# Whole 1 MB modulation tiles in a ring of two buffers in place of half tiles in a ring of four

## What is computed

```python
cond = jax.nn.silu(c)
mod = cond @ mod_w[i] + mod_b[i]                     # 2048 x 12288
sh_m, sc_m, gt_m, sh_f, sc_f, gt_f = jnp.split(mod[:, None, :], 6, axis=-1)
h = rms_norm(x, norm_g[i, 0]) * (1.0 + sc_m) + sh_m
y = swa_sink_attention(h, swa_w_qkv[j], swa_w_o[j], swa_sinks[j], cos, sin)
x = x + gt_m * rms_norm(y, norm_g[i, 1])
h = rms_norm(x, norm_g[i, 2]) * (1.0 + sc_f) + sh_f
x = x + gt_f * rms_norm(swiglu(h, ffn_w_in[i], ffn_w_out[i]), norm_g[i, 3])
```

## Time and profile before

| | |
|---|---|
| Median of three runs | 1232.06 us (1229.7 to 1233.01) |
| The profiled execution, its own time | 1226.82 us |
| Its span in the profile | 1225.0 us |
| Granted TensorE clock over the span | 0.933 |
| Busy: TensorE, VectorE, ScalarE, GpSimd | 86%, 64%, 39%, 7% of the span |
| Read from HBM | 286.39 MB, 235 GB/s over the span |

### The profile page before, as it was taken

The page is one execution under the profiler, slowest core; times in us unless marked ns, Lnnn a source line. Parts: engine busy times, 40 slices in busy tenths (PEclk is TensorE's granted clock), DMA queues, the critical chain, the costliest instruction groups (busy, mean ns, idle before and its releaser), DMA issues.

```text
span 1225.0 us, 13423 instructions
## 1 busy us (share of the span) xinstructions
PE 1053.1 (86%) x4712; PEld 862.1 (70%) x4712; DVE 782.4 (64%) x843; ACT 476.7 (39%) x568; POOL 83.5 (7%) x57
## 2 busy tenths in 40 slices
PE   0155568797778996999999999999999999999995
PEld 0144457576656765888888888888888888888884
DVE  5777879999987868476676644444444454454544
ACT  3311232653653444433343433343334434344343
POOL 0000013313311001000000000000000000000002
PEclk9677778798878998999999999999999999999998
DMA  8998877887779962687787755555655455555541
GB/s 310 362 322 308 297 273 249 282 307 274 267 251 341 342 241 68 205 293 265 268 303 278 268 178 194 185 199 176 205 174 201 149 198 202 178 202 194 185 169 69
DMA packets 104194, 288.94 MB, mean 236 GB/s; under 512 B 6752, under 2 KB 6752, under 8 KB 97888
## 3 DMA queue, kind: packets, MB, share of 16 engines
q1 hardware_dynamic: 103152, 286.29, 67.0%
q10 hardware_dynamic: 1008, 2.23, 0.5%
HBM read 286.39 MB, written 2.10 MB: 235 GB/s over the span
## 4 chain that ended last, share of the span: by engine, by line
PE 65%; DVE 16%; DMA 9%; issue 5%; ACT 4%; POOL 1%; ACTq 0%; SPq 0%; DVEq 0%
PE ps L1095 21%; PE ps L1097 21%; PE ps L1096 21%; DMA mraw<-in_mod_w 8%; DVE mraw L580 5%; DVE wlo L569 5%; ACT whi L312 2%; ACT s L368 1%; PE ps L1117 1%; DMA sinkp<-in_sinks 1%; DVE hf L842 1%; DVE qr L648 1%; PE ps L1214 0%; DVE qr L654 0%; PE ps L1234 0%
## 5 line engine op out<-in xcount | busy, mean ns | idle before, releaser
L569 DVE TENSOR_TENSOR wlo<-raw,whi 128x2048 fp32r<-128x2048 f32 x172 | 395.2, 2299 | 312.1 <-ACT whi L312 312.0
L1095 PE MATMUL ps<-whi,hThi 128*128 128x512 f32 x1248 | 497.6, 399 | 94.0 <-DVE wlo L569 88.7
L312 ACT ACTIVATE whi<-raw 128x2048 fp32r<-128x2048 f32 x172 | 328.7, 1913 | 466.5 <-PE ps L1097 455.7
L1096 PE MATMUL ps<-wlo,hThi 128*128 128x512 f32 x1248 | 492.9, 395 | 0.0
L1097 PE MATMUL ps<-whi,hTlo 128*128 128x512 f32 x1248 | 492.5, 395 | 0.0
L1095 PEld LDWEIGHTS ps<-whi,hThi 128*128 128x128 f32 x1248 | 238.9, 191 | 150.7 <-issue 91.1
L1097 PEld LDWEIGHTS ps<-whi,hTlo 128*128 128x128 f32 x1248 | 238.7, 191 | 50.9
L1096 PEld LDWEIGHTS ps<-wlo,hThi 128*128 128x128 f32 x1248 | 239.2, 192 | 49.2
L580 DVE CUSTOM_DVE_ANT_0 mraw<-mraw,cb,modT 128x1024 f32<-128x1024 f32 x96 | 128.7, 1358 | 36.0 <-DMA mraw<-in_mod_w 35.8
L580 DVE CUSTOM_DVE_ANT_0 mraw<-mraw,cb,mbias 128x1024 f32<-128x1024 f32 x96 | 124.3, 1311 | 41.2 <-DMA mraw<-in_mod_w 30.2
L1095 PE MATMUL ps<-whi,oThi 128*128 128x512 f32 x128 | 53.6, 419 | 6.3 <-DVE wlo L569 3.6
(11 more groups left out here) (131 smaller groups left out, 543.6 us busy)
## 6 DMA issues: line engine op xcount, KB each, us to landing
mraw<-in_mod_w SPq DMA_DIRECT2D x192, 512.0 KB, 6.2
raw<-in_w_in SPq DMA_DIRECT2D x88, 1024.0 KB, 5.1
raw<-in_w_out SPq DMA_DIRECT2D x44, 1024.0 KB, 4.8
raw<-in_w_qkv SPq DMA_DIRECT2D x24, 1024.0 KB, 8.7
raw<-in_w_o SPq DMA_DIRECT2D x16, 1024.0 KB, 8.5
x<-in_x ACTq DMA_DIRECT2D x2, 1024.0 KB, 11.9
x<-in_x SPq DMA_DIRECT2D x2, 1024.0 KB, 8.2
out<-x SPq DMA_DIRECT2D x8, 256.0 KB, 2.6
```

The lines of the kernel that those rows point to most:

```text
L312: A(whi[:, s % 2], raw[:, s], ACT.Copy).then_inc(hi_done, 1)
L569: V.tensor_tensor(wlo[:, s % 2], raw[:, s], whi[:, s % 2].bitcast(F32), ALU.subtract).then_inc(lo_done, 1)
L1095: mm(dst, hi, whi[:, s % 2, n], start=start, stop=False)
L1096: mm(dst, hi, wlo[:, s % 2, n], start=False, stop=False)
```

## The change

A modulation piece is a whole tile: one load of 128 rows of 8 KB, one multiply-and-sum over 2048 columns that starts from the bias. A group has four pieces f = 0 to 3. The ring has two buffers of 1 MB. The order written in terms of j stays as it is; a piece f stands where j = 2f stood, and at odd j nothing is done. So f0 to f3 stand at j = 0, 2, 4, 6. The load of a piece waits until VectorE has done the piece two before it. The wait of the second half for the first is gone.

```diff
-MHALF = D // 2
-MPN = 8
-MRING = 4
+MPN = 4
+MRING = 2
...
-        mraw = sb("mraw", [P, MRING, MHALF])
+        mraw = sb("mraw", [P, MRING, D])
...
-        def piece_of(j):
-
-            return 2 * (j // 4) + j % 2, j // 2 % 2
-
...
             def load_m(n, j, col=None, first=False):
 
-                if not first:
-                    sp.wait_ge(acc_step, MPN * n + j - 3)
+                if j % 2:
+                    return
+                f = j // 2
+                if not (first and f < MRING):
+                    sp.wait_ge(acc_step, MPN * n + f - 1)
                 c = n if col is None else col
-                f, half = piece_of(j)
-                src = mod_w[bass.ds(4 * c + f, 1), :, half * MHALF:(half + 1) * MHALF]
-                sp.dma_start(mraw[:, j % 4], src.rearrange("a p k -> p (a k)")).then_inc(m_loaded[j % 4], 16)
+                src = mod_w[bass.ds(4 * c + f, 1)].rearrange("a p k -> p (a k)")
+                sp.dma_start(mraw[:, f % 2], src).then_inc(m_loaded[f % 2], 16)
...
             def mod(n, j, col=None):
 
-                f, half = piece_of(j)
+                if j % 2:
+                    return
+                f = j // 2
                 c = n if col is None else col
                 dst = modT[:, bass.ds(4 * c + f, 1)]
-                dve.wait_ge(m_loaded[j % 4], 16 * (2 * n + j // 4 + 1))
-                if half:
-                    dve.wait_ge(acc_step, MPN * n + j - 1)
-                V.tensor_tensor_reduce(mraw[:, j % 4], mraw[:, j % 4], cb[:, half * MHALF:(half + 1) * MHALF],
-                                       1.0, dst if half else mbias[:, bass.ds(4 * c + f, 1)],
-                                       ALU.mult, ALU.add, dst).then_inc(acc_step, 1)
+                dve.wait_ge(m_loaded[f % 2], 16 * (2 * n + f // 2 + 1))
+                V.tensor_tensor_reduce(mraw[:, f % 2], mraw[:, f % 2], cb[:, :], 1.0,
+                                       mbias[:, bass.ds(4 * c + f, 1)], ALU.mult, ALU.add,
+                                       dst).then_inc(acc_step, 1)
```

More of the change, by code:

```diff
@@ L221, in _ @@
                 for u in range(2):
-                    for j in range(MPN):
+                    for j in range(8):
                         if (u, j) == (0, 2) and c:
```

## The result

The changed kernel takes 1249.37 us (median of four runs, 1247.34 to 1250.28) against 1232.09 us before (1229.7 to 1233.01): a ratio of 1.0141, with a 95% interval of 1.0121 to 1.0161. It is slower by 17.3 us; 14.5 were forecast. The profiled execution took 1248.68 us, span 1246.9 us, mean granted clock 0.933 as before.

The account below looks back on a forecast made before the run. Bounds: DMA queue and VectorE in turns up to 163 us, VectorE in attention, TensorE from the output projection. Terms 0 + 6 + 1.5 + 7 = +14.5 us on 1226.8 give 1241.3, as median 1246.5; range 1234 to 1257.

Parts of the forecast that it names:

- One tile on VectorE: On VectorE a whole tile steps in 2.27 us where two halves take 2.42, saving 0.15 us a tile.
- One tile on the queue: 1 MB lands after 4.8 us on an empty DMA queue; behind a full one, when the second half did.
- the queue rival: The DMA queue gains from fewer, longer transfers: -1 us for the whole kernel, about 1231 us; chance 0.12.
- A: Up to the first attention round (nine groups, 36 tiles): saved time is given back in bare landings; 0 us (-6 to +7).
- M+36.6: In the replay of one round of A, the next `acol` comes 36.6 us after M, the moment of `acol`.
- B: Four attention rounds: VectorE stalls 2.55 us for the third tile in each and `oT_lo` comes later; +6 us (0 to +10).
- C: Output projection: pieces wait longer for their buffer and multiply 1.06 us longer, little of it hidden; +1.5 us (-1 to +4).
- D: Four feed-forward blocks with modulation: subtracts come late and TensorE stands still; +7 us (+3 to +8).
- The saved VectorE time: Rival: B's 32 tiles and half of A's save 0.15 us each, -7, and TensorE hides D; 1225 us; chance 0.03.
- TensorE did not cool: Rival: new gaps in C and D drop TensorE to the 1.2 GHz level, +12 us on top, 1258 us; chance 0.10.

## Why the forecast held, and which step was wrong

**One tile on VectorE: right.** 2.27 to 2.28 us from one tile to the next (105.27 to 107.54, 297.82 to 300.10), as worked out.

**One tile on the queue: the landing right, the rule drawn from it too wide.** A bare megabyte lands in 4.7 us (4.8 taken). But against the queue rival I wrote that "there is no cost per transfer left to save", from two halves that landed 1.27 us apart behind a full queue. For a multiply that waits for the whole tile this step failed: a transfer less is worth some 0.2 us of queue time by the count alone and 0.3 with the longer rows, and the merged load is worth 31 us of kernel time. Where halves are multiplied as they land it stood: the merged load then gains nothing (1261.5 against 1258.7). The spacing of two landings behind a full queue shows the rate of bytes in flight; it does not show what the next load waits for before it is in flight. The rival was named with its right sign, at −1 us for the whole kernel. The parts of the change are larger than the whole: with the same transfers as before, the tile ring with one multiply costs +50 us (1280.3 against 1230.5), and the merged load takes 31 of it back; or, by the other runs, +4 for the order of halves, +24 for handling them by the tile, −9 for both merges. The prediction put down none of these. It used the landing of a whole megabyte (4.8 us) and the step of a whole multiply directly in each stage's replay, so they were in its lengths; a sum by separate effects would have missed. Part of the closeness is luck all the same: its terms stand against +21.9 us between the two profiled executions, and come near because the medians are only 17.3 apart.

The Trainium skill (DMA: Bandwidth & Descriptors, section Bandwidth) asks for batches of 1 MiB and more, from measurements of transfers that GpSimd issues; here SyncE does. The runs agree where one multiply waits for the tile (whole loads are 31 us faster) and not where halves are multiplied as they land (2.8 us slower). The change as a whole is slower.

**A: forecast 0, measured +3.1.** The replay itself was close: M+36.6 was worked out for the next `acol` and the third round shows 129.39 − 92.54 = 36.85, with f0 started at 121.95 (M+29.4, worked out M+29.1). VectorE in that round:

```profile
117.06 2.35 DVE L577 CUSTOM_DVE_ANT_0 mraw<-mraw,cb,mbias 128x2048 f32<-128x2048 f32 x1
...
121.95 2.35 DVE L577 CUSTOM_DVE_ANT_0 mraw<-mraw,cb,mbias 128x2048 f32<-128x2048 f32 x1 [2.53 <-DMA mraw<-in_mod_w]
...
127.12 2.35 DVE L577 CUSTOM_DVE_ANT_0 mraw<-mraw,cb,mbias 128x2048 f32<-128x2048 f32 x1 [2.81 <-DMA mraw<-in_mod_w]
```

What was missed is one round before it, whose last tile waited 3.55 us where this one waited 2.81; it is 2.8 us longer than before; the first `acol` was already 1.1 us late, and the last two rounds give 0.6 us back. The range for this term (−6 to +7) held it.

**B: forecast +6, measured +9.2.** Mechanism right, size off. The stall (2.47 us), `oTlo` and the maxima came where they were worked out. The rounds cost +1.4, +2.4, +3.9 and +1.5 us; the third alone goes past the +3 that I had as its upper end. In rounds two to four `oTlo` comes 2.5, 3.0 and 1.7 us later than before, and the round ends later by nearly that or more. The working had +2.75 for `oTlo` and then took only 1.7 for a round, as if some of it came back; it doesn't. The third round loses 0.9 us more behind the maxima, where a subtract waits 0.77 us for ScalarE's copy, and TensorE is busy 39.1 us in that round for the same 190 matmuls that took 35.9, at a granted clock of 0.86 against 0.93.

**C: forecast +1.5, measured +0.8.** Right in size, but not by its working. TensorE's waits for the subtracts in this stretch did not grow (1.46 us against 1.81). What differs is the start: TensorE stood idle 4.20 us for the last `oTlo` (2.08 before), and in the 9.8 us behind it the granted clock was 0.70, against 0.83.

**Between C and D: +1.3, not forecast.** No modulation runs there. All of it is one longer wait of VectorE for TensorE before the first `hf` (4.80 us in place of 3.53). From `acol` to `gu` the kernels with the tile ring take 72.8 to 73.3 us, all but one (half loads, whole multiply: 71.3). It isn't the ring's own: two kernels with half tiles take 72.0, but the one with its halves in the order of the tiles 72.9. The cause stays open.

**D: forecast +7, measured +7.5.** Right. Gaps of 0.31 and 0.92 us in the block shown, up to 1.4 in the others; seven in 186 us, 6.1 us in all, released by the subtract, none in the later blocks. Four blocks cost 1.5, 2.2, 1.6 and 2.2 us (1.7 each was taken). The run that only swaps the order of two loads takes all of it away.

**The other rivals.** The saved VectorE time did not carry: the engine has 20.8 us less to do and the kernel is longer. TensorE did not cool as that rival had it: the mean clock is 0.933 in both and 1.00 in the windows of C and D after. But it was lower in the third attention round and at the start of C, as told above; what part of B and C that is wasn't separated.

## What to carry to other kernels

Merging two pieces into one of double size is three changes: fewer and longer transfers, fewer instructions, and a coarser ring, in which one buffer only lies ahead. The coarser ring, with its coarser places in VectorE's order, was the loss here (24 us with loads and multiplies still by halves). The other two gained 9 us together and nothing apart, so test them as a pair and don't add up their prices. Price the ring by replaying a round with the bare landing time of the new size, and look at once at what mends it: another buffer, and asking for the piece before what is not needed as soon. Where a stage waits for loads, try one more buffer before changing the piece: here it gave the old kernel 13 us.

## What was not expected of the hardware

A second transfer for the same megabyte costs 0.31 us of queue time (825.8 against 795.5 us over 96), of which some 0.1 us goes with rows of 4 KB in place of 8 KB (805.5 us); with a third buffer in the first stage it costs 0.19 us (807.7 against 789.6). Each issue takes SyncE 0.33 us, near the same size; whether it is the cause wasn't separated. A multiply that needs the sum of the one just before it starts 0.11 to 0.14 us late. And the first of two transfers of 512 KB over 64 partitions each lands in the time of 1 MB over 128 (4.7 us).
